# Retention: the squares of a head are added in pairs on VectorE before the product with ones

## The reference

```python
def retention(xn, w_in, w_out):           # 4 heads, dk = 256, dv = 512, chunks of 128
    proj = xn @ w_in
    q, k, v, g = jnp.split(proj, ...)
    ...
    s = jnp.einsum('bihd,bjhd->bhij', qc, kc) * decay_mask[None]
    inner = jnp.einsum('bhij,bjhe->bihe', s, vc)
    ...
    out = rms_norm(out).reshape(B, S, H * dv)      # over the 512 values of a head
    return (jax.nn.silu(g) * out) @ w_out
```

## Time and profile before

| what | value |
|---|---|
| three runs | 1444.52, 1429.43 and 1444.54 us, median 1444.52 |
| profiled execution | 1431.53 us, of which the span of the trace is 1429.7 |
| TensorE busy | 1379.1 us, 96% of the span |
| VectorE, ScalarE, GpSimd busy | 65%, 48%, 14% |
| mean granted TensorE clock | 0.986 |
| retention's part with the table | about 785 to 862 us of the span |

### The profile page before, as it was taken

The page is one execution under the profiler, slowest core; times in us unless marked ns, Lnnn a source line. Parts: engine busy times, 40 slices in busy tenths (PEclk is TensorE's granted clock), DMA queues, the critical chain, the costliest instruction groups (busy, mean ns, idle before and its releaser), DMA issues.

```text
span 1429.7 us, 25085 instructions
## 1 busy us (share of the span) xinstructions
PE 1379.1 (96%) x9857; PEld 1275.0 (89%) x9857; DVE 925.5 (65%) x1181; ACT 690.3 (48%) x957; POOL 199.7 (14%) x137
## 2 busy tenths in 40 slices
PE   8999999989999999999999999999998988999998
PEld 7996988989998899988999997999987976899986
DVE  6876834465554677644864276788755676699963
ACT  5564353431213454433434545666645464666642
POOL 0000240004130000000000150122300000055510
PEclk9999999989999999999999999999999998999999
DMA  7442332420002555554454345455564540455552
GB/s 271 175 176 88 122 115 92 174 88 0 1 1 102 189 181 177 185 197 176 167 187 177 118 142 183 162 178 189 190 215 154 179 146 18 174 177 179 189 211 111
DMA packets 30315, 213.05 MB, mean 149 GB/s; under 512 B 3488, under 2 KB 3616, under 8 KB 5152
## 3 DMA queue, kind: packets, MB, share of 16 engines
q1 hardware_dynamic: 29088, 206.72, 40.8%
q0 software_dynamic: 1152, 5.24, 1.0%
HBM read 210.90 MB, written 1.05 MB: 148 GB/s over the span
## 4 chain that ended last, share of the span: by engine, by line
PE 88%; DVE 6%; ACT 3%; issue 2%; POOL 1%; DMA 0%; DVEq 0%; SPq 0%; POOLq 0%; ACTq 0%
PE lin L517 52%; PE lin L586 20%; PE aux L2074 2%; PE aux L2086 2%; PE aux L2084 1%; PE aux L2162 1%; PE aux L1969 1%; ACT whi L491 1%; PE lin L623 1%; POOL al L709 1%; PE aux L2174 1%; PE aux L2148 1%; DVE ro L1701 1%; PE aux L2272 1%; DVE iscore L1354 1%
## 5 line engine op out<-in xcount | busy, mean ns | idle before, releaser
L498 DVE TENSOR_TENSOR wlo<-raw,whi 128x2048 fp32r<-128x2048 f32 x182 | 419.4, 2308 | 189.9 <-ACT whi L491 189.6
L517 PE MATMUL lin<-xhi,whi 128*128 128x256 f32 (+1 forms) x1776 | 507.3, 286 | 2.3 <-DVE xlo L1269 1.8
L517 PE MATMUL lin<-xlo,whi 128*128 128x256 f32 (+1 forms) x1776 | 502.2, 283 | 0.0
L517 PE MATMUL lin<-xhi,wlo 128*128 128x256 f32 (+1 forms) x1776 | 500.0, 282 | 0.0
L491 ACT CAST whi<-raw 128x2048 fp32r<-128x2048 f32 x193 | 367.1, 1904 | 226.9 <-DMA raw<-in_stream 185.5
L517 PEld LDWEIGHTS lin<-xhi,whi 128*128 128x128 f32 x1776 | 334.0, 188 | 6.7 <-issue 5.4
L517 PEld LDWEIGHTS lin<-xhi,wlo 128*128 128x128 f32 x1776 | 336.6, 190 | 0.0
L517 PEld LDWEIGHTS lin<-xlo,whi 128*128 128x128 f32 x1776 | 334.8, 188 | 0.3
L684 POOL TENSOR_TENSOR wlo<-raw,whi 128x2048 fp32r<-128x2048 f32 x11 | 51.2, 4650 | 516.8 <-ACT whi L491 336.7
L1789 DVE SCALAR_TENSOR_TENSOR ft<-fy,par,ft 128x254 f32<-128x254 f32 (+1 forms) x176 | 96.3, 587 | 6.8 <-DVE ft L1789 1.7
L740 POOL TENSOR_TENSOR fu<-fs,ft 128x256 f32<-128x256 f32 x44 | 67.9, 1542 | 119.3 <-ACT fs L1196 119.3
(11 more groups left out here) (390 smaller groups left out, 2243.7 us busy)
## 6 DMA issues: line engine op xcount, KB each, us to landing
raw<-in_stream SPq DMA_DIRECT2D x193, 1024.0 KB, 4.9
gp<-in_gains POOLq DMA_DIRECT2D x6, 512.0 KB, 4.4
c<-in_const SPq DMA_DIRECT2D x1, 1652.0 KB, 18.2
h<-in_x SPq DMA_DIRECT2D x2, 544.0 KB, 4.2
c<-in_const POOLq DMA_DIRECT2D x1, 1024.0 KB, 5.2
ht<-in_xtok POOLq DMA_DIRECT2D x1, 1024.0 KB, 7.0
out<-ht SPq DMA_DIRECT2D x1, 512.0 KB, 2.6
out<-ht SPq DMA_DIRECT2D x2, 256.0 KB, 2.2
```

Source lines behind the costliest of these rows:

```text
L498: nc.vector.tensor_tensor(wlo[:, s0 % 4], raw[:, s0 % 4], whi[:, s0 % 4].bitcast(F32), ALU.subtract).then_inc(lo_ready, 1)
L517: ins = nc.tensor.matmul(out, a, b, start=start and n == 0, stop=stop and n == 2)
```

## The change

VectorE gets a new step, `pairs`: when ScalarE has squared both halves of a head, it adds tiles 2 and 3 of the squares onto tiles 0 and 1 (one addition of 128 x 512, in place). TensorE's `squares` then waits for that addition and makes two matmuls with ones where it made four. The new step stands in the table ahead of each `squares`.

```diff
+             ("pairs", 0), ("squares", 0), ("root", 0), ("product", 2), ("readout", 2), ("gate", 4), ("hi", 4), ("finish", 0),
+             ("pairs", 1), ("squares", 1), ("root", 1), ("product", 3), ("readout", 3), ("high", 0), ("gate", 5), ("hi", 5),
...
+            def pairs(hh):
+                after(dve, f"ro{hh}_0")
+                after(dve, f"ro{hh}_1")
+                q = rsq[:, hh % 2]
+                nc.vector.tensor_tensor(q[:, 0:2], q[:, 0:2], q[:, 2:4], ALU.add).then_inc(S("ro_pairs"), 1)
...
             def squares(hh):
-                after(pe, f"ro{hh}_0")
-                after(pe, f"ro{hh}_1")
+                pe.wait_ge(S("ro_pairs"), hh + 1)
                 b = fill(f"rn{hh}")
-                for e in range(4):
-                    ins = nc.tensor.matmul(b[:, 0:SEQ], ones[:], rsq[:, hh % 2, e], start=e == 0, stop=e == 3)
+                for e in range(2):
+                    ins = nc.tensor.matmul(b[:, 0:SEQ], ones[:], rsq[:, hh % 2, e], start=e == 0, stop=e == 1)
```

More of the change, by code:

```diff
@@ L94 @@
              ("gate", 2), ("hi", 2), ("silu", 2), ("product", 1), ("readout", 1), ("gate", 3), ("hi", 3), ("silu", 3),
[L95 to L98, removed]
+             ("pairs", 0), ("squares", 0), ("root", 0), ("product", 2), ("readout", 2), ("gate", 4), ("hi", 4), ("finish", 0),
+             ("pairs", 1), ("squares", 1), ("root", 1), ("product", 3), ("readout", 3), ("high", 0), ("gate", 5), ("hi", 5),
+             ("low", 0), ("finish", 1), ("pairs", 2), ("squares", 2), ("silu", 4), ("silu", 5), ("high", 1), ("gate", 6), ("hi", 6),
+             ("low", 1), ("root", 2), ("pairs", 3), ("squares", 3), ("finish", 2), ("gate", 7), ("hi", 7), ("root", 3), ("silu", 6),
              ("silu", 7), ("high", 2), ("finish", 3), ("low", 2), ("high", 3), ("low", 3)]
@@ L1707, in low @@
                     .then_inc(S("rlo"), 1)
-            todo = {"gate": gate, "finish": finish, "low": low}
+            todo = {"gate": gate, "pairs": pairs, "finish": finish, "low": low}
             for name, n in RETENTION:
```

## The result

The changed kernel takes 1458.2 us (median of 4 runs, 1454.4 to 1468.8) against 1437.3 us before (4 runs, 1429.4 to 1444.5). The ratio is 1.017, with a 95% interval from 1.012 to 1.023: slower, and by more than 1%; whether by 2%, these runs leave open. The profiled execution took 1458.75 us with a span of 1456.9; the one before had a span of 1429.7.

A forecast was written before the change was run, and what follows sets the result against it. TensorE was taken to bound the kernel, with VectorE's in-order list setting the end of this stretch. Waits 21.0, less 3.5 and 2.4, plus clock 6, gave +21 on 1437.5: about 1459 us, range 1443 to 1472.

The forecast's parts named there:

- The waits: TensorE at squares of heads 0 to 3: waits of 4.0, 5.6, 8.8 and 2.55 us, together 21.0 us.
- GpSimd's hold: GpSimd's weight subtraction stalls VectorE's two-SBUF-input addition at head 0: wait 4.0 us, without the hold 1.3.
- What is given back: At the output layer, TensorE's 2.44 us wait for rlo of head 2 goes; removed matmuls save 3.46 us.
- sum without the clock: Whole kernel: 21.0 - 3.5 - 2.4 = 15.1 us slower.
- The cover of 5 us: After gate slot 7: VectorE needs 0.64 + 4.2 + 1.2 = 6.1 us while TensorE runs 11.3 us of output layer.
- the list of signs: Expected profile after: four waits, squares at 0.87 us, rlo wait gone, output layer some 15 us later plus clock.
- The clock: TensorE's clock halves behind the three long gaps: 2 us each, 6 us, bounds 0 and 12.
- Rival 1: Waits at squares as summed, but clock stays up: +15, 1446.5 to 1459.5 us, middle 1453; chance 0.2.
- rival 2: Clock comes back slower, 4 us for each of three gaps: +27, 1458.5 to 1471.5 us, middle 1465; chance 0.12.
- Rivals 3 and 4: At squares: additions directly follow gate steps, -0.6 us, chance 0.06; or nothing waits, nothing to -3.5 us, chance 0.03.
- The level: Base for the whole kernel: 1437.5 us, middle of four executions at two levels; plus 21 gives about 1459.

The follow-up runs named there:

- The experiments with a tiny step: Changed kernel with the pair step cut to one column, squares with four matmuls again; profiled executions 1456.4 us (two SBUF inputs) and 1459.1 us (one).
- the one with one input: Changed kernel, pair step reduced to one column times a constant, reading one SBUF input, four matmuls in squares; profiled execution 1459.1 us.
- the waits filled: Changed kernel with 16, 23, 37 and 10 small matmuls of ones on TensorE ahead of its waits at squares; ratio to before 1.016.
- the kernel with early additions: Changed kernel with each pair addition moved right behind the readout of its head in VectorE's list; ratio to before 1.000.

## Why the prediction was right

**The waits.** Predicted 4.0, 5.6, 8.8 and 2.55 us, measured 3.93, 5.57, 8.76 and 2.52. The experiments with a tiny step show that the place in the list makes them, and the one with one input that GpSimd's hold was 2.5 us of the first. The sum of waits came as worked out because every piece was read from a row of before, in the order in which the new list has them.

**What is given back.** 3.5 us of matmuls and 2.4 us of waiting: sum without the clock +15.1, measured +15.7 with the waits filled. The cover of 5 us held: `rlo` of head 2 ended at about 881.8 (the first of two that begin at 880.56), and TensorE, which began the output layer at 875.57, needed it 11.3 us later, at about 886.9. One reading in the list of signs was wrong by its own terms: the 2.4 us of waiting lie behind the start of the output layer, so that start moves by 21.0 - 3.5 = 17.5 us without the clock and not by 15. With the waits filled it moved by 18.3, in the changed kernel by 27.6, both counted from the first score matmul.

**The clock.** This is the term that was mis-sized: 6 us taken, 9.3 measured. I charged three gaps with 2 us each. It fell behind all four, the 2.5 us one too, and on average by 2.3 us each. The 2.44 us gap of before, which left the clock alone, was no guide for one of 2.52 us here, though those of 1.67 to 1.99 us in the experiments left it alone again. The rule on idle gaps of the Trainium skill, page "TensorE: Matmul & The Clock Gate", section "Why this matters for your kernels", fits the three long gaps, behind each of which the clock fell; on gaps as short as 2.44 and 2.52 us it says nothing. The low clock is also why the four rows of `squares` came at 2.07 us and not at the 0.87 that the prediction listed. The sum was 21 for a stretch that grew by 25.0, of a span that grew by 27.2. Rival 1 (the clock stays up) is out; rival 2, +27, was nearer in size than the forecast, but its 4 us a gap is not what happened either. Rivals 3 and 4 are out by the first wait alone.

**The level.** 1459 against 1458.2 is closer than the sum was, and that is luck. The forecast added 21 to 1437.5, the middle of the two levels at which its four executions lay. Of the 48 runs of before that came with the timed experiments 34 lie at 1429 to 1432 and 14 at 1438 to 1448, so the common level is the lower one, and from there the change costs about 26 us (the three lower runs of the changed kernel are at 1454 to 1459). A term too small and a base too high cancelled. That the medians of the result are 20.9 us apart, next to my 21, is chance too: two of its four runs of before were at the upper level, and one of the four of the changed kernel.

## What to carry to other kernels

On an engine that works through its list in order, an added step costs what stands in front of it, not what it takes itself: here 0.69 us of addition made 5.6 and 8.8 us of waiting, and behind the readouts, ahead of the gate steps on which the waiting hung, it was free. Before a product is halved, look which engine ends the stretch: here 3.5 us of matmuls were worth nothing until VectorE's list had been shortened, and 3.5 us of this stretch afterwards. When a new wait falls on TensorE, price the clock too: here 9.3 us on top of 15.7.

## What the runs showed of the hardware

The upper of the two levels of time shows up in a trace. The profiled execution of the kernel with early additions took 1447.2 us, some 15 more than its runs at the lower level, and the row of its busy time by stretch says where:

```profile
202.00:228.00 26.00, 26.00 (x104) 21.80 (x104) 2.04 (x8) 5.42 (x12) 7.71 (x2) 0.50 0.12 41
```

The same stretch before the change:

```profile
202.00:228.00 26.00, 26.00 (x186) 22.36 (x186) 3.40 (x12) 11.11 (x22) 6.52 (x2) 1.00 0.19 62
```

With TensorE busy throughout in both, 104 matmuls were done at 0.50 and 186 at 1.00. This part of the program is the same in both kernels, and at the first score matmul this execution is 12.8 us later than the one before the change (792.6, not 779.8). Why the clock stays low there in some executions was not tried, and that the other executions at the upper level have the same cause is argued from the size alone.

A fall of the clock behind a gap lasted from some 3 us (behind the 2.52 us gap: 0.50 in 868 to 870, 1.00 in 871) to 6 us of TensorE's work (behind the 3.93 us gap), and the length of the gap did not order them: behind the longest, 8.76 us, it was 5.
